# Odd experts' up weights issued by GpSimd on a queue of their own

## The reference

```python
def moe(h, w_router, b_router, w_up, b_up, w_down, b_down):
    logits = (t @ w_router + b_router)
    top_v, top_i = lax.top_k(logits, 4)
    gates = jax.nn.softmax(top_v, axis=-1)
    ...
    for each expert e, for the tokens routed to it:
        uu = xb @ w_up[e] + b_up[e]                 # 1024 x 2048
        glu = min(uu[:, :1024], 7); lin = clip(uu[:, 1024:], -7, 7)
        act = glu * sigmoid(1.702 * glu) * (lin + 1)
        y[tokens] += gate * (act @ w_down[e] + b_down[e])   # 1024 x 1024
```

## Time and profile before

| | us |
|---|---|
| median of 3 runs | 1204.15 |
| lowest and highest run | 1202.72, 1205.23 |
| profiled execution | 1201.8 |
| its span, first to last instruction | 1199.7 |
| PE busy | 1147.0 (96%) |
| VectorE, ScalarE, GpSimd busy | 401.8, 298.9, 36.3 |
| moved by DMA | 444.75 MB |

### The profile page before, as it was taken

One profiled execution on the slowest core, in us unless ns is written; L12 is line 12 of the kernel. 1 busy time (PEld: TensorE's weight loads), 2 busy tenths in 40 slices (PEclk: granted clock), 3 DMA queues, 4 the chain that ended last, 5 costly groups with the idle time before them and its releaser, 6 DMA issues.

```text
span 1199.7 us, 14539 instructions
## 1 busy us (share of the span) xinstructions
PE 1147.0 (96%) x5685; PEld 543.9 (45%) x5685; DVE 401.8 (33%) x702; ACT 298.9 (25%) x481; POOL 36.3 (3%) x88
## 2 busy tenths in 40 slices
PE   7999999988999999999999999899989999999995
PEld 5889699863333333333333333233333333333332
DVE  5445584632232223132323332122222232313134
ACT  6752543431111111111121111111111111111113
POOL 2005300000000000000000000000000000000000
PEclk9999999999999999999999999899999999999998
DMA  9930435498999999999999999999999999999993
GB/s 359 339 153 1 195 141 193 190 397 346 367 428 428 428 428 428 428 428 429 428 428 428 429 428 429 429 428 429 428 428 428 429 428 428 429 428 428 427 427 153
DMA packets 35375, 444.75 MB, mean 371 GB/s; under 512 B 4084, under 2 KB 4660, under 8 KB 7568
## 3 DMA queue, kind: packets, MB, share of 16 engines
q1 hardware_dynamic: 25840, 319.56, 63.8%
q10 hardware_dynamic: 8496, 121.66, 23.9%
q0 software_dynamic: 1008, 3.09, 0.7%
HBM read 440.57 MB, written 3.73 MB: 370 GB/s over the span
## 4 chain that ended last, share of the span: by engine, by line
PE 95%; DVE 2%; another core or an unknown queue 2%; DMA 1%; ACT 0%; issue 0%; SPq 0%; DVEq 0%; ACTq 0%
PE ps L454 38%; PE ps L468 19%; PE ps L331 15%; PE ps L431 7%; PE ps L461 3%; PE ps L475 2%; PE ps L476 2%; PE ps L437 2%; PE ps L446 1%; PE ps L1723 1%; DMA regionB<-in_w_mk 1%; PE ps L1773 1%; PE ps L1785 1%; PE ps L443 1%; PE ps L482 0%
## 5 line engine op out<-in xcount | busy, mean ns | idle before, releaser
L454 PE MATMUL ps<-regionB,regionP 128*64 128x512 f32 x1024 | 238.4, 608 | 13.4 <-DMA regionB<-in_w_up 13.4
L454 PE MATMUL ps<-regionA,regionP 128*64 128x512 f32 x1024 | 224.6, 594 | 7.1 <-DMA regionA<-in_w_up 6.3
L468 PE MATMUL ps<-regionD,regionP 128*64 128x512 f32 x992 | 225.0, 595 | 0.0
L747 DVE TENSOR_TENSOR regionP<-ps,regionP 128x512 f32<-128x512 f32 x32 | 22.1, 691 | 401.9 <-PE ps L437 401.9
L454 PEld LDWEIGHTS ps<-regionA,regionP 128*64 128x64 f32 x1024 | 71.6, 137 | 148.7 <-issue 136.1
L454 PEld LDWEIGHTS ps<-regionB,regionP 128*64 128x64 f32 x1024 | 69.0, 138 | 146.7 <-issue 130.2
L468 PEld LDWEIGHTS ps<-regionD,regionP 128*64 128x64 f32 x992 | 68.4, 137 | 129.0 <-issue 129.0
L741 DVE SCALAR_TENSOR_TENSOR roundedP<-regionP,roundedP 64x512 fp32r<-64x512 f32 x62 | 43.8, 747 | 158.5 <-ACT roundedP L625 158.5
L640 ACT ACTIVATE regionP<-ps 128x512 f32<-128x512 f32 x31 | 18.5, 597 | 298.2 <-PE ps L431 298.2
L431 PE MATMUL ps<-regionP 128*64 128x512 f32 x384 | 90.3, 606 | 1.2 <-DVE regionP L707 1.2
L781 DVE TENSOR_TENSOR regionP<-ps,regionP 128x1024 f32<-128x1024 f32 (+1 forms) x48 | 58.5, 1220 | 95.7 <-PE ps L476 85.1
(11 more groups left out here) (292 smaller groups left out, 1114.5 us busy)
## 6 DMA issues: line engine op xcount, KB each, us to landing
regionA<-in_w_up SPq DMA_DIRECT2D x64, 2048.0 KB, 41.8
regionB<-in_w_up SPq DMA_DIRECT2D x64, 2048.0 KB, 43.6
regionD<-in_w_down ACTq DMA_DIRECT2D x58, 2048.0 KB, 14.1
regionD<-in_w_down SPq DMA_DIRECT2D x4, 2048.0 KB, 18.0
regionD<-in_w_mv SPq DMA_DIRECT2D x4, 1024.0 KB, 20.9
regionD<-in_w_out SPq DMA_DIRECT2D x4, 1024.0 KB, 11.2
regionD<-in_w_mq SPq DMA_DIRECT2D x4, 1024.0 KB, 4.8
regionD<-in_w_mo SPq DMA_DIRECT2D x4, 1024.0 KB, 4.8
```

The costliest lines, as they stand in the source:

```text
L454: ins = pe.matmul(ps[64 * half:64 * half + 64, n_, :], XTe[:, k % 4, k // 4, :], w[:, k, 1024 * half + 512 * n_:1024 * half + 512 * n_ + 512],
L468: ins = pe.matmul(ps[64 * n_:64 * n_ + 64, at_bank, :], rows[:, k, :], w[:, k, 512 * n_:512 * n_ + 512], start=(k == 0), stop=(k == KT - 1))
```

## The change

SP keeps the up quarters of the even experts. Those of the odd experts are issued by GpSimd, in a loop of its own (`moe_pool`) behind the last of its other instructions, each quarter on the same `up_done` count as before. They signal new semaphores, `later_upB_in0` to `later_upB_in3`; the first load of `upB` (expert 1), which SP still issues, keeps `upB_in`. PE's wait ahead of a quarter names the semaphore that belongs to it. `down_30(0)`, which stood ahead of the last quarter of expert 31 on SP, now stands behind SP's loop. Outside of the expert part, pairs of semaphores are merged into one with counts to match (`gate_exp` and `gate_ln` into `gate_log`, `gx1H` and `sq1` into `gx1`, `smax` and `nmax` into `score_max`, `rinv` into `probs`).

```diff
@@ moe_sync
             def one(e, h, pair, first, last):
                 if isinstance(e, int) and e + 2 >= E:
                     return
+                if h == 1:
+                    return
                 for c_ in range(4):
-                    if isinstance(e, int) and e == E - 3 and c_ == 3:
-                        down_30(0)
                     sp.wait_ge(S("up_done"), e * 4 + c_ + 1)
-                    sp.dma_start((upA, upB)[h][:, 2 * c_:2 * c_ + 2, :], up_src(e + 2)[:, 2 * c_:2 * c_ + 2, :]
-                                 ).then_inc(S(f"up{'AB'[h]}_in{c_}"), 16)
+                    sp.dma_start(upA[:, 2 * c_:2 * c_ + 2, :], up_src(e + 2)[:, 2 * c_:2 * c_ + 2, :]
+                                 ).then_inc(S(f"upA_in{c_}"), 16)
             over_experts(sp, one)
+            down_30(0)
             down_30(1)
...
+        def moe_pool(pool):
+            def one(e, h, pair, first, last):
+                if h == 0 or last:
+                    return
+                for c_ in range(4):
+                    pool.wait_ge(S("up_done"), e * 4 + c_ + 1)
+                    pool.dma_start(upB[:, 2 * c_:2 * c_ + 2, :], up_src(e + 2)[:, 2 * c_:2 * c_ + 2, :]
+                                   ).then_inc(S(f"later_upB_in{c_}"), 16)
+            over_experts(pool, one)
...
@@ moe_tensor
-                    pe.wait_ge(S(f"up{'AB'[h]}_in{c_}"), (pair + 1) * 16)
+                    if h == 0:
+                        pe.wait_ge(S(f"upA_in{c_}"), (pair + 1) * 16)
+                    elif second:
+                        pe.wait_ge(S(f"upB_in{c_}"), 16)
+                    else:
+                        pe.wait_ge(S(f"later_upB_in{c_}"), pair * 16)
...
@@ gpsimd
             pool.partition_all_reduce(small[:, 131:132], nover, P, bass.bass_isa.ReduceOp.max).then_inc(S("nover"), 1)
+            moe_pool(pool)
```

More of the change, by code:

```diff
@@ L1099, in _ @@
                 has(act, f"gate{j}")
-                act.activation(v_, v_, ACT.Exp, scale=-1.0).then_inc(S("gate_exp"), 1)
-                act.wait_ge(S("gate_exp"), j + 1)
-                act.activation(v_, v_, ACT.Ln, bias=1.0).then_inc(S("gate_ln"), 1)
+                act.activation(v_, v_, ACT.Exp, scale=-1.0).then_inc(S("gate_log"), 1)
+                act.wait_ge(S("gate_log"), 2 * j + 1)
+                act.activation(v_, v_, ACT.Ln, bias=1.0).then_inc(S("gate_log"), 1)
             act.wait_ge(S("wu_in"), 16)
@@ L1161, in _ @@
                 has(act, f"out{k}")
-                act.activation(gxH[:, k, :], xT[:, k, :], ACT.Copy, scale=g_memq[:, k:k + 1]).then_inc(S("gx1H"), 1)
-                act.activation(sq1[:, k, :], xT[:, k, :], ACT.Square).then_inc(S("sq1"), 1)
+                act.activation(gxH[:, k, :], xT[:, k, :], ACT.Copy, scale=g_memq[:, k:k + 1]).then_inc(S("gx1"), 1)
+                act.activation(sq1[:, k, :], xT[:, k, :], ACT.Square).then_inc(S("gx1"), 1)
                 if k in (3, 5, 7):
@@ L1172, in _ @@
                 took(act, f"s{j}")
-                act.wait_ge(S("nmax"), m + 1)
+                act.wait_ge(S("score_max"), 2 * m + 2)
                 for h2 in range(2):
@@ L1306, in _ @@
                 free(dve.tensor_tensor(kT[:, j, :], bank(f"k{j}", NT), rstdb[:, :], ALU.mult), f"k{j}")
-            dve.wait_ge(S("gate_ln"), 2)
+            dve.wait_ge(S("gate_log"), 4)
             for j, (i0, ni, n) in enumerate(((0, 2, P), (2, 1, 64))):
@@ L1420, in low_queries, with add_square @@
             def low_queries(k):
-                dve.wait_ge(S("gx1H"), k + 1)
+                dve.wait_ge(S("gx1"), 2 * k + 1)
                 dve.scalar_tensor_tensor(gxL[:, k, :], xT[:, k, :], g_memq[:, k:k + 1], gxH[:, k, :].bitcast(F32),
                                          ALU.mult, ALU.subtract).then_inc(S("gx1L"), 1)
-            def add_square(k, sq, square, total):
-                dve.wait_ge(S(square), k + 1)
+            def add_square(k):
+                dve.wait_ge(S("gx1"), 2 * k + 2)
                 if k > 1:
-                    dve.wait_ge(S(total), k - 1)
-                dve.tensor_tensor(sq[:, 0, :], sq[:, 0, :], sq[:, k, :], ALU.add).then_inc(S(total), 1)
+                    dve.wait_ge(S("sqsum1"), k - 1)
+                dve.tensor_tensor(sq1[:, 0, :], sq1[:, 0, :], sq1[:, k, :], ALU.add).then_inc(S("sqsum1"), 1)
             for k in range(KT):
@@ L1434, in _ @@
                 if k > 1:
-                    add_square(k - 1, sq1, "sq1", "sqsum1")
+                    add_square(k - 1)
                 if k in (4, 6):
@@ L1438, in _ @@
             low_queries(7)
-            add_square(7, sq1, "sq1", "sqsum1")
+            add_square(7)
             low_square(6)
@@ L1458, in normalise @@
                 c0 = score_col(j)
-                dve.reciprocal(rinv[:, c0:c0 + 2], rs[:, c0:c0 + 2]).then_inc(S("rinv"), 1)
-                dve.wait_ge(S("rinv"), m + 1)
+                dve.reciprocal(rinv[:, c0:c0 + 2], rs[:, c0:c0 + 2]).then_inc(S("probs"), 1)
+                dve.wait_ge(S("probs"), 3 * m + 1)
                 for h2 in range(2):
@@ L1467, in _ @@
                 dve.tensor_reduce(mx[:, c0:c0 + 2], bank(f"s{j}").rearrange("p (h m) -> p h m", h=2), AX.X,
-                                  ALU.max).then_inc(S("smax"), 1)
-                dve.wait_ge(S("smax"), m + 1)
+                                  ALU.max).then_inc(S("score_max"), 1)
+                dve.wait_ge(S("score_max"), 2 * m + 1)
                 dve.tensor_scalar(nmx[:, c0:c0 + 2], mx[:, c0:c0 + 2], rs1n[:, j // 2:j // 2 + 1], None,
-                                  ALU.mult).then_inc(S("nmax"), 1)
+                                  ALU.mult).then_inc(S("score_max"), 1)
                 if m >= 2:
@@ L1787, in values @@
                 end(ins)
-            pe.wait_ge(S("probs"), 6)
+            pe.wait_ge(S("probs"), 9)
             turn("PT4", [(256 * h + 128 * i, probs_s[:, h, 128 * i:128 * i + 128], P, P) for h in range(2) for i in range(2)])
@@ L1802, in _ @@
             values(0)
-            pe.wait_ge(S("probs"), 10)
+            pe.wait_ge(S("probs"), 15)
             turn_probs(2)
```

## The result

The changed kernel takes 1221.53 us (median; 1220.43 to 1222.54), the kernel before, measured beside it, 1204.69 us (1202.72 to 1206.79). The ratio is 1.0141, with a 95% interval of 1.0128 to 1.0153: **16.8 us slower**. The profiled execution took 1222.54 us, its span 1220.6 us.

The account below looks back on a forecast made before the run. PE sets the pace to about 740 us, DMA after; time is PE's work plus 25.7 us of waits. Waits become 38.1, +12.4: profiled 1201.8 becomes 1214.2, plus 2.35 gives a median of 1216.5, range 1208 to 1236.

Parts of the forecast that it names:

- Equal shares: Queues with work share the engines equally; with three, the ACT queue's down weights go from 214 GB/s to 142.7.
- Place and name of the waits: PE waits at the down product on regionD, odd experts 7 to 27, some 3.7 us a pair; none on up quarters.
- First late load: Expert 7's down load is the first late one, 1.5 us, then ten at 3.66: waits of 38.1 us.
- the window: Odd experts' time from first down issue to PE's use of the second half: 26.2 us, up to 5.6 late.
- the prediction's own rule: Odd down load: 1.72 MB in 8.05 us, 2.47 MB at a third in 17.3, plus 2.35 fixed: 27.7 us.
- The fixed part of a load: Of the 4.8 us that a 1024 KB load alone takes, 2.45 is moving and 2.35 fixed.
- The tail: After PE's last wait, experts 29 to 31 remain; last byte lands at about the same time; waiting earlier costs +12.4 us.
- Zero for the issue time, the merged semaphores and the order of `down_30`: GpSimd's issue of 0.73 us against 0.33 on SP, merged semaphores, and upB's last quarter issued earlier: each worth 0.
- A median landing well over 14.1: Sign of the forecast: the down loads' median time from issue to landing lies well over 14.1 us.
- Small packets: Rival, 17%: GpSimd's transfers go in small packets, odd quarters late instead of down halves: +18.2 (1222) or +30 (1234).
- No change: Rival, 7%: same 428 GB/s, PE's waits only change their names, and the time stays 1204.
- Faster: Rival, 6%: odd quarters stop waiting in line, the 13.4 us of waits on upB go, time 1191.

Follow-up runs that it names:

- the two runs that cost nothing: Against the kernel before: all later up quarters issued by GpSimd, 1204.46 us against 1204.59; merged semaphores and moved `down_30(0)` with SP issuing all up quarters, 1204.30 against 1204.77.

## Why the prediction was right, and where its size was off

*Equal shares: right.* The queues of the changed kernel from 507 to 511 us, when all three held work:

```profile
q0 software_dynamic: 38, 0.62, 36.5%
q10 hardware_dynamic: 40, 0.57, 33.7%
q1 hardware_dynamic: 34, 0.56, 32.6%
```

Three thirds, where the earlier trace rows had two halves. The Trainium skill ("DMA: Bandwidth & Descriptors", Queues, rings and completion order) says that an engine goes round between the queues that have work, one packet a turn. The packet counts agree: 38, 40 and 34.

*Place and name of the waits: right.* Down halves of odd experts to expert 27, none on up quarters, 428 GB/s. GpSimd's queue carries 128.93 MB, of which 60 x 2.097 = 125.8 are the moved quarters.

*First late load, and so the size: too small.* The prediction had expert 7's as the first, 1.5 us late, then ten at 3.66: 38.1. Measured are 2.1 for expert 5 (its pair takes 57.21), 3.6 for expert 7 (58.76), and for the ten pairs after it 589.9 - 551.3 = 38.6 (from 555.65 to 1145.53): 44.3. Of the 6.2 us missing, 4.2 are the first two. The step that failed is the window, the time that an odd expert's down weights have: 26.2 us was read from the loop of expert 30, and that loop was itself stretched by a wait of 1.0 us for an up quarter ahead of 1134.97. In a loop without waits (expert 5's weights; ScalarE's issue and PE's use of the second half) the kernel before shows

```profile
432.86 3.76 ACTq L654 DMA_DIRECT2D regionD<-in_w_down  x2
```

```profile
457.54 3.65 PE L468 MATMUL ps<-regionD,regionP 128*64 128x512 f32 x16
```

457.54 - 432.86 = 24.7 us. (The 4.2 us to spare at a half were too many as well: this second half, issued at 436.28, landed 20.1 us later, 1.2 us ahead of its use.) By the prediction's own rule, with that window, expert 7's load is 27.7 - 24.7 = 3.0 us late. Expert 5's has 3.6 MB of upB beside it: 1.72 MB of it at a half in 8.05 us, 1.88 at a third in 13.2, the last 0.59 at a half again in 2.8, and 2.35: 26.3 us, 1.6 late. The sum is then 1.6 + 3.0 + 36.6 = 41.2, and the forecast 3.1 us nearer. In the changed kernel the same load is issued at 435.48 and PE begins at 462.25:

```profile
435.48 3.76 ACTq L670 DMA_DIRECT2D regionD<-in_w_down  x2
```

```profile
462.25 3.65 PE L479 MATMUL ps<-regionD,regionP 128*64 128x512 f32 x16 [2.02 <-DMA regionD<-in_w_down]
```

Landed 26.7 us after the issue, 2.0 late: the rule came close, and its window was wrong. Of the 3.1 us that are left, 2.0 are the ten later pairs, 38.6 instead of 36.6. DMA was not slower. From PE's restart behind expert 7's late half to the one behind expert 27's,

```profile
521.00 3.65 PE ps L479 x16
...
1109.18 5.35 PE ps L479 x16
```

ten pairs take 588.2 us, 58.82 each, where the prediction put 58.80. What is left of the 2.0, 1.7 us, is the row behind the last wait, 5.35 us at a granted clock of 0.68 instead of 3.65: no later wait makes up for it. The prediction had no such term. It read PE's slow rows in the kernel before as waits that lie inside a matmul row; at 756.89 the row ran at a clock of 0.55. The last 1.1 us, in the first two late loads, stay open.

*The fixed part of a load: off, with little effect here.* 2.35 us was taken from a load with nothing beside it. Under load it is about twice that (next section but one). Against that, upB moves 1.47 MB alone before the down load's first packet (the q0 line further below), which is then no longer beside it, and the upA quarter that comes to compete starts as late (issued at 443.52, first packet at 447.0). How nearly these cancel isn't worked out. That the rule came out within half a microsecond is luck in part, for it knew none of them.

*The tail: price right, DMA's end wrong.* Table by stretches (as in rows 2), the changed kernel:

```profile
1146.00:1158.00 12.00, 12.00 (x58) 4.02 (x56) 4.66 (x8) 2.07 (x4) 0.00 (x0) 1.00 1.00 426
1158.00:1166.00 8.00, 8.00 (x40) 2.72 (x36) 0.00 (x0) 0.60 (x1) 0.00 (x0) 1.00 0.14 57
...
1176.00:1188.00 12.00, 12.00 (x53) 4.17 (x53) 4.28 (x4) 0.94 (x4) 0.00 (x0) 1.00 0.99 416
```

And the kernel before:

```profile
1158.00:1166.00 8.00, 8.00 (x38) 2.74 (x34) 2.10 (x2) 0.74 (x4) 0.00 (x0) 1.00 1.01 430
...
1176.00:1188.00 12.00, 11.06 (x50) 4.04 (x47) 4.70 (x8) 5.82 (x9) 0.00 (x0) 1.00 0.14 58
```

Here the lead turns into loss. After the last wait (expert 27's, near 1109) PE still has more than three experts of work, DMA runs out of up weights and moves 57 GB/s from 1158 to 1166, where it used to move 430; what is left to load waits for PE and is done some 10 us later than before. The prediction had DMA full to the same time, and it isn't; but the price that it set for waiting earlier, the difference of the waits, is the one the table of all kernels bears out.

*Zero for the issue time, the merged semaphores and the order of `down_30`: right*, by the two runs that cost nothing. *A median landing well over 14.1: a sign badly chosen.* It is 15.6, and inside the loop the median even fell; the second halves of the odd experts show the third share (above).

*The rivals.* Small packets: GpSimd's queue alone on the engines moves full ones (435.5 to 438.9 us):

```profile
q0 software_dynamic: 92, 1.47, 101.8%
```

1.47 MB in 92 packets is 16 KB each, at 432 GB/s. No change: the rate is indeed the same, but the shares decide what comes late. Faster: it needed 435 GB/s, and the highest slice in the expert loop has 430.

## What to carry to other kernels

Where DMA is nearly full, a queue is a share: before a stream gets a queue of its own, name the stream whose share it cuts, and ask whether that one has a second buffer. Serve loads in the order in which they are wanted; a load that arrives early on a full engine makes another one late, and a lead that is still there when the last load is issued is time lost. Read a deadline from a loop without waits, since one that waits shows more room than there is. And before a long row of PE is called a wait, read the granted clock in it: here rows just behind a wait ran at the lower level.

## What the runs showed of the hardware that was not expected

**A down load's first packet comes 3.4 us after its issue under load.** ScalarE issues at 435.48 (above), and from 435.5 to 438.9 the ACT queue (q10) has no packet: the list of queues for that stretch has only the q0 line shown above. It isn't the new queue's doing, for the kernel before has the same after its issue at 432.86. Its queues from 432.9 to 436.2 us:

```profile
q1 hardware_dynamic: 90, 1.44, 102.5%
```

So it is at every first down half from expert 2 to 29 in the kernel before, 3.4 to 3.6 us each. At expert 1's, issued at 322.31 when the engines were almost idle (36 GB/s from 322.3 to 323.2), it is 1.0.

At the other end, of the load that PE could use at 462.25, the changed kernel's queues from 461.1 to 463.9:

```profile
q1 hardware_dynamic: 87, 1.23, 103.1%
q10 hardware_dynamic: 2, 0.00, 0.0%
```

Its data had gone by 461.1, 1.1 us ahead. Together that is 4.5 us an expert in which the single down buffer gets no data, where a whole 1024 KB load with nothing beside it lands in 4.8. The Trainium skill ("DMA: Bandwidth & Descriptors", Latency and other measured facts) gives about 0.6 us to the first byte for such a queue; with the engines full, the trace does not agree.

**GpSimd's queue is an equal of the other two** for 2048 KB loads with rows of 16 KB: 16 KB packets, a third of the engines beside two full queues, all of them alone, and no cost in time that shows with 120 transfers on it.
